# A routed feed-forward layer's expert weights, loaded in whole matrices of 8 MB and 4 MB in place of halves

## The reference

```
h   = rmsnorm(x + merged @ w_out)
w   = softmax(top 4 router logits of h)
for each of a token's four experts e:
    gu  = h @ w_gu[e] + b_gu[e]             # 1024 x 2048: 8 MB
    g   = min(gu[:1024], 7);  lin = clip(gu[1024:], -7, 7)
    y  += w[e] * (((lin + 1) * g * sigmoid(1.702 g)) @ w_down[e] + b_down[e])   # 1024 x 1024: 4 MB
out = rmsnorm(x + y)
```

## Time and profile before

| | |
|---|---|
| median of 3 runs | 1184.27 us (1183.45 to 1184.77) |
| the profiled execution's own time | 1183.07 us |
| its span, first to last instruction | 1181.3 us |
| mean granted TensorE clock | 0.981 |
| TensorE (PE) busy | 1105.3 us, 94% |
| DVE, ACT, POOL busy | 33%, 21%, 0% |
| moved by the DMA engines | 452.13 MB, mean 383 GB/s |
| expert loads issued by SP | 50 of 4096 KB, 58 + 17 of 2048 KB, 22 + 11 of 1024 KB, 2 of 512 KB |

### The profile page before, as it was taken

The page is one execution under the profiler, slowest core; times in us unless marked ns, Lnnn a source line. Parts: engine busy times, 40 slices in busy tenths (PEclk is TensorE's granted clock), DMA queues, the critical chain, the costliest instruction groups (busy, mean ns, idle before and its releaser), DMA issues.

```text
span 1181.3 us, 14726 instructions
## 1 busy us (share of the span) xinstructions
PE 1105.3 (94%) x6066; PEld 584.6 (49%) x6066; DVE 392.6 (33%) x650; ACT 245.6 (21%) x388; POOL 4.5 (0%) x10
## 2 busy tenths in 40 slices
PE   9999999999999989898898989898999989998996
PEld 8999999983443333333333333333343333333332
DVE  7768655563222322222222222222222222222222
ACT  5444774432111111111111111111111111111113
POOL 0000000000000000000000000000000000000000
PEclk9999999999999999999999999999999999999999
DMA  9955754689999999999999999999999999999996
GB/s 331 324 179 188 263 168 151 258 326 413 425 424 429 431 432 428 429 434 433 429 427 438 428 428 428 437 429 427 428 437 431 426 431 428 430 431 429 412 423 266
DMA packets 61131, 452.13 MB, mean 383 GB/s; under 512 B 3570, under 2 KB 34535, under 8 KB 40871
## 3 DMA queue, kind: packets, MB, share of 16 engines
q1 hardware_dynamic: 60272, 449.53, 92.1%
q0 software_dynamic: 560, 1.74, 0.5%
q10 hardware_dynamic: 263, 0.34, 0.1%
HBM read 450.53 MB, written 1.06 MB: 382 GB/s over the span
## 4 chain that ended last, share of the span: by engine, by line
PE 49%; DMA 48%; DVE 1%; issue 0%; SPq 0%; ACT 0%; DVEq 0%
DMA dring<-in_w_down_dram 41%; PE bank L1182 19%; PE bank L1557 13%; PE bank L1506 10%; DMA ring<-in_w_gu_dram 7%; PE bank L1451 1%; PE bank L1189 1%; PE bank L1396 1%; PE bank L1277 0%; PE bank L1426 0%; PE bank L1518 0%; PE bank L1460 0%; DMA region_x<-in_mem_dram 0%; PE bank L1623 0%; PE bank L1298 0%
## 5 line engine op out<-in xcount | busy, mean ns | idle before, releaser
L1506 PE MATMUL bank<-ring,region_x 128*64 128x512 f32 x2048 | 456.3, 597 | 7.2 <-DMA ring<-in_w_gu_dram 7.2
L1557 PE MATMUL bank<-dring,region_r 128*64 128x512 f32 x1024 | 247.4, 634 | 55.4 <-DMA dring<-in_w_down_dram 54.9
L1506 PEld LDWEIGHTS bank<-ring,region_x 128*64 128x64 f32 x2048 | 141.0, 137 | 280.1 <-issue 264.3
L1557 PEld LDWEIGHTS bank<-dring,region_r 128*64 128x64 f32 x1024 | 74.2, 145 | 225.6 <-issue 135.1
L1182 PE MATMUL bank<-hT_high,w_high 128*128 128x256 f32 x384 | 109.9, 286 | 0.0
L1182 PE MATMUL bank<-hT_low,w_high 128*128 128x256 f32 x384 | 108.6, 283 | 0.0
L1182 PE MATMUL bank<-hT_high,w_low 128*128 128x256 f32 x384 | 108.6, 283 | 0.0
L755 DVE TENSOR_TENSOR w_low<-ring,w_high 128x2048 fp32r<-128x2048 f32 x38 | 87.0, 2289 | 51.7 <-ACT w_high L488 51.6
L1089 DVE TENSOR_SCALAR region_r<-bank 128x512 f32<-128x512 f32 x32 | 22.1, 692 | 245.2 <-PE bank L1506 245.2
L1108 DVE SCALAR_TENSOR_TENSOR y_parts<-bank,region_r,y_parts 64x512 fp32r<-64x512 f32 x31 | 23.1, 744 | 214.5 <-ACT y_parts L656 214.5
L639 ACT ACTIVATE region_r<-region_r 128x512 f32<-128x512 f32 x32 | 20.1, 630 | 315.3 <-DVE region_r L1089 315.3
(11 more groups left out here) (250 smaller groups left out, 880.1 us busy)
## 6 DMA issues: line engine op xcount, KB each, us to landing
ring<-in_w_gu_dram SPq DMA_DIRECT2D x50, 4096.0 KB, 25.7
dring<-in_w_down_dram SPq DMA_DIRECT2D x58, 2048.0 KB, 24.4
ring<-in_w_gu_dram SPq DMA_DIRECT2D x17, 2048.0 KB, 12.0
ring<-in_w_in_dram SPq DMA_DIRECT2D x26, 1024.0 KB, 6.6
ring<-in_w_gu_dram SPq DMA_DIRECT2D x22, 1024.0 KB, 8.5
dring<-in_w_down_dram SPq DMA_DIRECT2D x11, 1024.0 KB, 11.6
ring<-in_w_out_dram SPq DMA_DIRECT2D x4, 1024.0 KB, 4.8
ring<-in_w_mem_kv_dram SPq DMA_DIRECT2D x3, 1024.0 KB, 11.8
```

Source lines behind the costliest of these rows:

```text
L1506: last = mm(ps[64 * half:64 * half + 64, :], xg[u // 2][:, c, 64 * (u % 2):64 * (u % 2) + 64], ring[:, slot0 + c, k * F + half * 512:k * F ...
L1557: last = mm(ps[64 * half:64 * half + 64, :], lhsT, dring[:, c // 2, at:at + 512], start=(c == 0), stop=(c == KC - 1))
```

## The change

- The layout goes from fours to eights: chunk k holds row 8p + k. A whole up matrix is then one transfer with 64 KB per partition, a whole down matrix one with 32 KB. Halves and pairs are now rows of 32 KB and 16 KB that stand 64 KB and 32 KB apart.
- Tables say how each matrix is cut. Up matrices 9 to 21 come whole (8 MB), 5 to 8 and 22 to 29 in halves; down matrices 8 to 19 whole (4 MB), 1 to 7 and 20 to 29 in two pairs. The others are cut as before, except that chunks 6 and 7 of experts 0 and 1 come one by one and each one mixer piece earlier than the pairs did.
- For a whole matrix SP waits until all eight chunks (four slots) of the former one are used, and TensorE waits for the whole before its first product.
- The hidden values are transposed with 16 products of 64x64 against the identity in place of four 128x128 transposes, behind the scatter matrix's two instead of ahead of them.
- The first tokens have a buffer of their own (the place of `y_parts`), and the first `start_sum(1, 0)` runs behind the up products of expert 0 instead of ahead of them.
- The loops of SP and TensorE cover fewer experts; more of them are written out.

The diff, cut to its core:

```diff
+SINGLES = tuple((c, 1) for c in range(KC))
+PAIRS = tuple((c, 2) for c in range(0, KC, 2))
+UP_RUNS = {0: PAIRS[:3] + SINGLES[6:], 1: PAIRS[:3] + SINGLES[6:], 2: SINGLES, 3: SINGLES,
+           4: SINGLES[:4] + PAIRS[2:], E - 2: PAIRS, E - 1: PAIRS[:3] + SINGLES[6:]}
+DOWN_RUNS = {0: SINGLES[:4], 1: PAIRS[:2], E - 2: SINGLES[:4], E - 1: SINGLES[:4]}
+UP_RUNS.update({e: ((0, 4), (4, 4)) for e in (*range(5, 9), *range(E - 10, E - 2))})
+DOWN_RUNS.update({e: PAIRS[:2] for e in (*range(2, 8), *range(E - 12, E - 2))})
+def up_runs(e):
+    return UP_RUNS.get(e, ((0, 8),))
+def down_runs(e):
+    return DOWN_RUNS.get(e, ((0, 4),))
...
         def up_chunks(expert, slot, c, n):
-            m, k = c // 4, c % 4
             sp.dma_start(ring[:, slot:slot + n, :].rearrange("p k n -> p (k n)"),
-                         a["w_gu"][0, bass.ds(expert, 1), m * 512:(m + 1) * 512, :]
-                         .rearrange("e (p k) n -> p (e k n)", k=4)[:, k * PIECE:(k + n) * PIECE]).then_inc(piece_in[slot], 16)
+                         a["w_gu"][0, bass.ds(expert, 1), :, :]
+                         .rearrange("e (p k) n -> p (e k n)", k=KC)[:, c * PIECE:(c + n) * PIECE]).then_inc(piece_in[slot], 16)
...
-        for c in range(0, KC, 2):
-            sp.wait_ge(pieces_used, N_MIX - MIX_RING + 1 + c)
-            up_chunks(1, c, c, 2)
+        for c, n in up_runs(1):
+            sp.wait_ge(pieces_used, N_MIX - MIX_RING + c + n - 1)
+            if c > 5:
+                up_chunks(0, 8 + c, c, n)
+            up_chunks(1, c, c, n)
             if c == 2:
                 down_slots(0, 0, 1)
                 down_slots(0, 1, 1)
-        up_chunks(0, 14, 6, 2)
...
-        with sp.Fori(0, more * (E // 2) + (E // 2 - 8)) as i:
-            expert_up((i * 2 + 6) % E, 8, i * 16 + (N_MIX - RING + 49))
-            expert_down((i * 2 + 4) % E, i * 8 + 13)
-            expert_up((i * 2 + 7) % E, 0, i * 16 + (N_MIX - RING + 57))
-            expert_down((i * 2 + 5) % E, i * 8 + 17)
+        whole_up, whole_down = ((0, 8),), ((0, 4),)
+        with sp.Fori(0, more * (E // 2) + (E // 2 - 10)) as i:
+            expert_up((i * 2 + 10) % E, 8, i * 16 + (N_MIX + 8 * KC + 1), whole_up)
+            expert_down((i * 2 + 8) % E, i * 8 + (8 * DRING + 1 - DRING), whole_down)
+            expert_up((i * 2 + 11) % E, 0, i * 16 + (N_MIX + 9 * KC + 1), whole_up)
+            expert_down((i * 2 + 9) % E, i * 8 + (9 * DRING + 1 - DRING), whole_down)
...
-            dve.tensor_tensor(xg[0][:, 2 * n:2 * n + 2, :],
+            dve.tensor_tensor(first_xg[:, 2 * n:2 * n + 2, :],
...
         gather_quarter(0)
-        start_sum(1, 0)
...
-        def hidden_transposed(s, halves):
-            pe.wait_ge(hid_ready, s + 1)
-            pe.wait_ge(xg_sb, s + halves)
-            for c in range(4):
-                last = transpose(tr_ps[:, c * P:(c + 1) * P], g_sb[:, c * P:(c + 1) * P], ident)
+        def hidden_transposed():
+            for c in range(KC):
+                for m in range(2):
+                    half = slice(64 * m, 64 * m + 64)
+                    last = mm(tr_ps[half, 64 * c:64 * c + 64], g_sb[half, 64 * c:64 * c + 64], ident[half, half],
+                              start=True, stop=True)
             last.then_inc(hidT_done, 1)
...
             s = i * 4 + u
-            hidden_transposed(s, halves)
+            pe.wait_ge(hid_ready, s + 1)
+            pe.wait_ge(xg_sb, s + halves)
             pe.wait_ge(y_ready, s + 1)
             slots_transposed(s, y_ps)
+            hidden_transposed()
             scatter_of(s - 1, (u + 1) % 2)
...
-        up(0, 0, False, {0: second_quarter, 2: third_quarter, 3: lambda: gather_quarter(3)}, True)
+        up(0, 0, 0, {0: second_quarter, 2: third_quarter, 3: lambda: gather_quarter(3)}, True)
+        start_sum(1, 0)
         begin(1)
```

More of the change, by code:

```diff
@@ L77, in loads_before, with up_landed, down_landed @@
     return sum(mixer_slot(q) == slot for q in range(N_MIX))
+SINGLES = tuple((c, 1) for c in range(KC))
[9 more added lines that the diff above has]
+    return DOWN_RUNS.get(e, ((0, 4),))
+def up_landed(e, c):
+    return sum((c in dict(up_runs(x))) for x in range(e % 2, e + 1, 2))
+def down_landed(e, j):
+    return sum((j in dict(down_runs(x))) for x in range(e + 1))
 C_ID, C_TRI, C_SLOT, C_HALF, C_PICK = 0, P, 2 * P, 3 * P, 4 * P
@@ L355, in _, with expert_up @@
         sp.dma_start(x_again, a["x"][0].rearrange("(t p) d -> p t d", p=P)).then_inc(x_again_in, 16)
-        def expert_up(expert, slot0, uses, n=4):
-            for c in range(0, KC, n):
+        def expert_up(expert, slot0, uses, runs):
+            for c, n in runs:
                 sp.wait_ge(pieces_used, uses + c + n - 1)
@@ L363, in down_slots, with expert_down @@
         def down_slots(expert, j, n):
-            m, k = j // 2, j % 2
             sp.dma_start(dring[:, j:j + n, :].rearrange("p k n -> p (k n)"),
[L367 to L372, removed]
+                         a["w_down"][0, bass.ds(expert, 1), :, :]
+                         .rearrange("e (p k) n -> p (e k n)", k=KC)[:, j * PIECE:(j + n) * PIECE]).then_inc(down_in[j], 16)
+        def expert_down(expert, uses, runs):
+            for j, n in runs:
                 sp.wait_ge(downs_used, uses + j + n - 1)
@@ L461, in _ @@
         pool.dma_start(b_rt, a["b_router"].broadcast_to([P, E])).then_inc(router_in, 16)
[L462 to L463 removed]
+        pool.dma_start(g_eights, bass.AP(a["rows"].tensor, 16 * P, [[KC, P], [1, KC]])).then_inc(g_eights_in, 16)
     @block.scalar
@@ L1484, in begin, with up @@
             bias_rows(1)
-        def up(i, u, last_one, between, first=False):
+        def up(i, u, e, between, first=False):
             s = i * 4 + u
             slot0 = 8 if u % 2 == 0 else 0
+            tokens = first_xg if e in (0, 1) else xg[u // 2]
             for c in range(KC):
@@ L1537, in small_products, with down @@
             s = i * 4 + u
-            hidden_transposed(s, halves)
+            pe.wait_ge(hid_ready, s + 1)
+            pe.wait_ge(xg_sb, s + halves)
             pe.wait_ge(y_ready, s + 1)
             slots_transposed(s, y_ps)
+            hidden_transposed()
             scatter_of(s - 1, (u + 1) % 2)
-        def down(s, single, ps=y_ps, between=None):
+        def down(s, e, ps=y_ps, between=None):
             pe.wait_ge(hidT_sb, s + 2)
@@ L1549, in down @@
             for c in range(KC):
-                if c % 4 == 0:
+                if c % KC == 0:
                     pe.wait_ge(down_in[c // 2], (s + 1) * 16)
-                elif c % 2 == 0:
-                    pe.wait_ge(down_in[c // 2], 16 + 16 * single)
-                lhsT = hidT[:, (c % 4) * P + 64 * (c // 4):(c % 4) * P + 64 * (c // 4) + 64]
+                elif c % 2 == 0 and e is not None and c // 2 in dict(down_runs(e)):
+                    pe.wait_ge(down_in[c // 2], 16 * down_landed(e, c // 2))
+                lhsT = hidT[:, 64 * c:64 * c + 64]
                 for half in range(2):
@@ L1560, in down @@
                     last.then_inc(downs_used, 1)
-                if single == 2 and c == KC - 2:
+                if e == E - 1 and c == KC - 2:
                     pe.wait_ge(last_slot_in, 16)
@@ L1608, in _ @@
         for u in range(1, 4):
-            one_expert(0, u)
+            one_expert(0, u, u)
+        for u in range(4):
+            one_expert(1, u, 4 + u)
         more = pe.value_load(more_i32[0:1, 0:1], min_val=0, max_val=PASSES - 1)
-        with pe.Fori(0, more * (E // 4) + (E // 4 - 2)) as i:
+        with pe.Fori(0, more * (E // 4) + (E // 4 - 4 - 1)) as i:
             for u in range(4):
-                one_expert(i + 1, u)
+                one_expert(i + 2, u, None)
+        for g in range(E // 4 - 3, E // 4 - 1):
+            for u in range(4):
+                one_expert(more * (E // 4) + g, u, 4 * g + u)
         i = more * (E // 4) + (E // 4 - 1)
@@ L1624, in _ @@
                            start=False, stop=False)
-            down(s, u // 2)
+            down(s, E - 4 + u)
             if u < 2:
```

104 lines of the change are left out of this document (50 added, 54 removed).

## The result

The changed kernel takes **1199.54 us** (median of 4 runs, 1197.44 to 1199.72), beside 1184.02 for the kernel before on the same chip (4 runs, 1183.45 to 1184.77): ratio 1.013, 95% interval 1.0118 to 1.0142. It is slower by some 15.5 us and lies outside the range that I gave. Two executions further on, one of the old layout in halves and one of the first mixed kernel, took 1385 us at a granted clock of 0.75 and are left out of their ratios. The profiled execution has a span of 1195.6 us, 14.3 more than that of before.

The account below looks back on a forecast made before the run. From about 274 us to the last down matrix, DMA bytes divided by rate bound the kernel. Terms -1.6 + 1.3 + 1.05 - 0.35 = +0.4 us on 1184.27 gave 1184.7 us, range 1181.0 to 1190.5.

Parts of the forecast that it names:

- Part 2: Middle loop: whole matrices wait for all eight chunks and full landing; queue just holds, +1.3 us (0 to +6.9).
- latency of 1.45 us: Last product to up issue 0.2 us, issue to first packet 0.9, last packet to landing 0.35.
- 29.1 us of queue: Work queued, up e+3 and down e+1, while TensorE finishes up e+2: 29.22 - 2 x 0.06.
- Rival (a): Queue runs dry before whole up matrices in cold periods: +6.9 us, total 1190.3; chance 0.23.
- The fixed 2.0 us: Skill's cost per transfer, tried in place of 1.25 us of latency: cold case dry by 0.75, +4 us in all.
- The cold penalty: Clock falls after idle ahead of down products, +1.74 or +3.0 us each, in every second period; a dry spell shortens the next idle.
- Part 1: 25 fewer, larger transfers in a full queue, 0.06 us each: -1.6 us (-2.8 to 0).
- Rival (b): Cover holds and each transfer costs 0.11 us: -2.8 us, total 1181.5; chance 0.27.
- rival (c): 64 KB rows are cut in two by hardware, so up matrices gain nothing: -0.8 instead of -1.6, 1185.5; chance 0.08.
- Part 3: Hidden transposes as 16 64x64 products: +0.8 us per expert, covered in the middle, +1.05 us at the end (+0.3 to +1.8).
- Part 4: Front: single chunks 6 and 7 and later start_sum let the first product start earlier: -0.35 us (-0.5 to 0).
- What costs nothing: Gain columns' transfer, stride of eights, first tokens' buffer, waits and written-out loops' code: put at 0.

Follow-up runs that it names:

- the old layout in halves: Changed kernel's front, small-product order and unrolled loops, but four rows per partition, 128x128 transposes, all matrices in halves and pairs: 1185.88 us, 1.0016 to the kernel before.
- the first mixed kernel: Up matrices whole in 64 KB rows through expert 28, down matrices in pairs of 32 KB rows with the old transposes: 1187.12 us, 1.0028 to the kernel before.
- The two runs with a filler: Changed kernel plus three discarded products ahead of each whole down matrix: 1197.32 us; with less TensorE work per expert and five such products: 1185.57 us.
- the two runs: Changed kernel with only up matrices 9 to 21 whole: 1187.51 us, 1.0032; with only down matrices 8 to 19 whole: 1188.20 us, 1.0036.
- the run with 32 KB rows: Old layout and transposes under the changed kernel's order, up 9 to 21 in one 8 MB transfer of 256 rows, down in pairs: 1186.29 us, 1.0021.
- the rolled run: Old layout in halves under the changed kernel's order, with TensorE's loop running over experts 8 to 27: 1185.11 us, 1.0013 to the kernel before.

## Why the prediction was wrong

**Part 2 is the step that failed**, at the latency of 1.45 us. TensorE's side was right: warm, I had 25.1 + 0.8 + 0.2 = 26.1 from down product to issue, and the trace gives 26.4; cold, 27.7 to 29.4. What I then set against 29.1 us of queue was 0.9 us to the first packet and 0.35 from the last, as if sixteen engines were one that may work until the last moment. A warm period would leave a lead of 29.06 - 26.37 = 2.7 us; the need is 3.5 us where the engines end close together and over 5 where they don't. The two runs with a filler show it: both at a granted clock of 1.00 over the middle with all waits of the changed kernel, one with leads of mostly 2.7 to 4.2 us and a mean of 30.10 over eleven periods, the other with 5.2 and (855.31 - 534.67) / 11 = 29.15. Price: 0.84 us in each of 11 periods, where I had 1.3 us in all. Rival (a), to which I gave 0.23, named the mechanism, but with the same 1.45 us its 6.9 were too few as well.

The need has three parts, by the packets. First, the issue must come 2.5 us ahead of the end of the first engine: 0.97 us to its first packet, as I had it (0.9), and beyond that the first packets, which take some 3.1 us for 2.42. Second, the spread of the engines' ends, 0.5 to 4.4 us, which I had at nothing. Third, 0.3 to 0.7 us from the last end to the product, for which I had 0.35. The Trainium skill, "DMA: Bandwidth & Descriptors", section "Why a DMA increments its semaphore by 16 and not by 1", says that the engines finish independently and only the full count means landed. The traces agree.

The fixed 2.0 us of the Trainium skill, "DMA: Bandwidth & Descriptors", section "Anatomy of one DMA", which I had set in place of my 1.25, would have moved the sum the right way and stopped short: the measured need is larger than both.

**The cold penalty** I had right in kind. The down products took up to 10.05 us, and with a cold one the lead is gone. But I expected it to be self-correcting (a dry spell shortens the next idle). It isn't: the dry spell delays the landing after it, so that idles of 0.38 and 5.39 us take turns, and each 5.39 brings a cold product and the next dry spell. Keeping the clock alone gave back only some 2 us (1199.54 to 1197.32). Nor does the length of the idle tell by itself whether the clock falls: in the kernel before, 2.45 us ahead of the product of 557.52 cost nothing, while 2.31 ahead of that of 674.38 did (8.78 us).

**Part 1**: one transfer in a full queue cost 0.06 by the sum (25 times that is 1.5, not 1.6), 0.08 by the periods of the two runs; but it is the row length that pays, as the run with 32 KB rows shows. My fit was one of c per transfer or per row and could not tell. Rival (b), c = 0.11, and rival (c), by the packets, are out. **Part 3**: from the start of the small products to the next up products it is 908.89 - 906.31 = 2.58 us for 892.95 - 891.22 = 1.73, +0.85 (I said +0.8), and TensorE's unwaiting period is 25.92 (said 25.9). At the end +0.9 (said +1.05). What failed is that I counted them at the end alone: they cost 2.9 us scaled from the kernel before, 3.2 by the old transposes. From 300 to 420 us TensorE hardly waits for memory and itself releases the stream (the down products of expert 0 start at 308.43 for 307.86, those of expert 3 at 388.00 for 384.92), so each 0.8 us is late in the queue too. **Part 4**: the first product piece was to start 0.35 us earlier and starts 0.06 earlier (271.20 for 271.26). It stands closer behind the first `start_sum` by 0.43, but that one starts at 268.38 for 268.01. The hole moved as said, from the window 240 to 270 us into the next (share 0.99 and 0.95 there, for 0.85 and 1.00); by 300 us 78.5 MB have moved for 78.7. Worth nothing. **What costs nothing**: the loops written out, put at 0, cost some 0.6 us in the old layout, with 40 packets of code for 32 (the changed kernel has 46, the kernel before 28). Some 1.5 us between the rolled run and the kernel before stay without a cause.

Step by step through the runs: before 1183.9, small products +3.2, written-out loops +0.6, the rest of the new order +1.5, the waiting at both ends +10.3 (net of what the longer rows save). That these make up the 1199.5 is no test, as they are differences of one chain of runs.

## What to carry to other kernels

When a ring is refilled in one transfer that waits for its last slot, count the lead from the issue to the end of the work still queued on the engine that is through first, not only whether the queue is "not empty", and not to the landing, which the last engine sets. Here, with 64 KB packets, it took 2.5 us to the first engine's end, and up to 4.4 us lay between the first and the last. Joining transfers at both ends of a ring (a late release and a late landing) can cost far more than either alone; try them singly, and ask what pays, the number of transfers or the row length. Work that hides under a wait in one stretch may be on the path in another, and an engine freed of work gives part of it back to its clock if it then idles.

## What I had not expected of the hardware

- Sixteen first packets behind some 2 us without a start took 3.12 us on average, against 2.42 in a running queue.
- The sixteen engines end one 4 MB transfer 0.54 to 4.38 us apart, and only the last end counts as the landing.
- Leaving out 2.6 us of TensorE work per expert brought the issue forward by only 0.6 us on average (25.8 for 26.4), since idles of 3.0 to 8.9 us left the down products at 8.4 to 10.0 us; a filler that burns five products in the idle brought back the other 1.9 (23.9) and 8 us of the whole.
- An 8 MB transfer of 256 rows of 32 KB is worth nothing over two of 4 MB (1186.29 for 1185.88, periods of 29.22 us in both), while 128 rows of 64 KB give 0.08 us each (29.14).
